# Reading the moving operand of a split product in alternating steps of 16 columns

## Time and profile before

| | |
|---|---|
| median of 3 runs | 2075.34 us (2073.47 to 2078.24) |
| profiled execution, its own time | 2075.21 us |
| its span, first to last instruction | 2073.4 us |
| PE busy | 1975.6 us, 95% of the span |
| PEld busy | 1644.3 us, 79% |
| DVE busy | 1725.3 us, 83% |
| ACT busy | 1328.1 us, 64% |
| read from memory | 557 MB, 269 GB/s over the span |
| mean granted TensorE clock | 0.982 of full |

### The profile page before, as it was taken

How to read it: one execution, slowest core, us unless ns; L and a number is a source line. 1 busy time by engine, 2 the same in 40 slices (tenths; PEclk the granted TensorE clock), 3 DMA queues, 4 the chain that set the end, 5 groups by cost and what they waited for, 6 DMA issues and landing times.

```text
span 2073.4 us, 28446 instructions
## 1 busy us (share of the span) xinstructions
PE 1975.6 (95%) x10316; PEld 1644.3 (79%) x10316; DVE 1725.3 (83%) x2440; ACT 1328.1 (64%) x1977; POOL 0.2 (0%) x4
## 2 busy tenths in 40 slices
PE   6998999989989999999999999999999998999997
PEld 5777889978877788788888878888888876767785
DVE  7798878768776698989989898998989988785764
ACT  4353534355564587788788787888878774554543
POOL 0000000000000000000000000000000000000000
PEclk9999999999999999999999999999999999999999
DMA  9856689846332298999999999999989994672630
GB/s 378 300 170 234 229 301 327 287 142 207 116 111 82 91 382 325 359 334 382 366 351 365 329 368 345 374 352 340 371 325 377 380 354 158 222 247 68 217 122 21
DMA packets 154211, 560.19 MB, mean 270 GB/s; under 512 B 17232, under 2 KB 17488, under 8 KB 153936
## 3 DMA queue, kind: packets, MB, share of 16 engines
q1 hardware_dynamic: 154064, 558.29, 74.1%
HBM read 557.18 MB, written 1.05 MB: 269 GB/s over the span
## 4 chain that ended last, share of the span: by engine, by line
PE 78%; DVE 12%; ACT 5%; issue 3%; DMA 2%; DVEq 0%; SPq 0%; ACTq 0%
PE ps L527 22%; PE ps L529 22%; PE ps L528 22%; PE ps L533 10%; DVE spl L516 3%; PE ps L537 3%; DVE macc L580 2%; ACT sph L504 2%; DMA ring<-in_hyb_w_in 1%; DVE arena L2169 1%; DMA ring<-in_dense_down 1%; ACT arena L771 1%; ACT arena L2135 0%; DVE hL L884 0%; ACT ps L890 0%
## 5 line engine op out<-in xcount | busy, mean ns | idle before, releaser
L504 ACT ACTIVATE sph<-ring 128x1024 fp32r<-128x1024 f32 x906 | 949.2, 1059 | 517.0 <-PE ps L529 332.8
L516 DVE TENSOR_TENSOR spl<-ring,sph 128x1024 fp32r<-128x1024 f32 x906 | 1078.2, 1219 | 241.5 <-ACT sph L504 229.0
L527 PE MATMUL ps<-sph,hH 128*128 128x512 f32 (+1 forms) x1296 | 522.6, 403 | 1.4 <-DVE hL L884 1.3
L529 PE MATMUL ps<-sph,hL 128*128 128x512 f32 (+1 forms) x1296 | 507.8, 392 | 0.0
L528 PE MATMUL ps<-spl,hH 128*128 128x512 f32 (+1 forms) x1296 | 506.9, 391 | 0.0
L529 PEld LDWEIGHTS ps<-sph,hL 128*128 128x128 f32 x1296 | 245.5, 189 | 52.6
L527 PEld LDWEIGHTS ps<-sph,hH 128*128 128x128 f32 x1296 | 246.4, 190 | 51.3 <-issue 3.8
L528 PEld LDWEIGHTS ps<-spl,hH 128*128 128x128 f32 x1296 | 246.4, 190 | 48.4 <-issue 1.0
L527 PE MATMUL ps<-sph,rH 128*128 128x512 f32 x664 | 269.1, 405 | 5.9 <-ACT arena L3123 2.3
L529 PE MATMUL ps<-sph,rL 128*128 128x512 f32 x664 | 259.9, 391 | 0.0
L528 PE MATMUL ps<-spl,rH 128*128 128x512 f32 x664 | 259.4, 391 | 0.0
(11 more groups left out here) (317 smaller groups left out, 1754.4 us busy)
## 6 DMA issues: line engine op xcount, KB each, us to landing
ring<-in_moe_gu SPq DMA_DIRECT2D x448, 512.0 KB, 5.4
ring<-in_moe_down SPq DMA_DIRECT2D x224, 512.0 KB, 5.3
ring<-in_mod SPq DMA_DIRECT2D x144, 512.0 KB, 5.0
ring<-in_w_in SPq DMA_DIRECT2D x64, 512.0 KB, 4.5
ring<-in_dense_gu SPq DMA_DIRECT2D x44, 512.0 KB, 5.3
ring<-in_ssm_w_in SPq DMA_DIRECT2D x40, 512.0 KB, 4.2
ring<-in_dense_down SPq DMA_DIRECT2D x22, 512.0 KB, 5.4
ring<-in_hyb_w_in SPq DMA_DIRECT2D x20, 512.0 KB, 5.9
```

Of the source, the lines that this page charges most:

```text
L504: a.activation(k.high[m % SPLITS][:, 0:w], raw[:, 0:w], ACT.Copy).then_inc(k.S.half_rounded, 1)
L516: v.tensor_tensor(k.low[m % SPLITS][:, 0:w], raw[:, 0:w], k.high[m % SPLITS][:, 0:w], ALU.subtract).then_inc(*k.tick(k.S.half_split, f"hal ...
L527: pe.matmul(out, a[0], b[0], start=start, stop=False, skip_group_check=True)
L529: return pe.matmul(out, a[1], b[0], start=False, stop=stop, skip_group_check=True)
```

## The change

`mm3` passes the output and the two moving operands through a new function `paced`. Where the width is a multiple of 256, it reads the columns in another order: the operand is cut in two halves (`j`), each half in steps of 16 columns (`n`), and the steps are taken from the last to the first, at each of them the one of the lower half and then the one of the upper half. Inside a step the 16 columns go upwards. For 512 columns the order is 240 to 255, 496 to 511, 224 to 239, 480 to 495, and so on to 0 to 15, 256 to 271. The output gets the same order, so that each column of the product lands where it did. At 296 columns nothing changes. The stationary operand, the number of matmuls, all waits, counters and transfers, and the products by `mm` and `turn` stay as they are.

```
+def paced(ap):
+
+    return ap.rearrange("p (j n i) -> p n j i", j=2, i=16)[:, ::-1] if ap.shape[1] % 256 == 0 else ap
+
+
 def mm3(pe, out, a, b, start, stop):
-    pe.matmul(out, a[0], b[0], start=start, stop=False, skip_group_check=True)
-    pe.matmul(out, a[0], b[1], start=False, stop=False, skip_group_check=True)
-    return pe.matmul(out, a[1], b[0], start=False, stop=stop, skip_group_check=True)
+    out, high, low = paced(out), paced(b[0]), paced(b[1])
+    pe.matmul(out, a[0], high, start=start, stop=False, skip_group_check=True)
+    pe.matmul(out, a[0], low, start=False, stop=False, skip_group_check=True)
+    return pe.matmul(out, a[1], high, start=False, stop=stop, skip_group_check=True)
```

## The result

| | before | after |
|---|---|---|
| median of 9 runs | 2073.47 us (2068.16 to 2078.24) | 2089.64 us (2079.18 to 2096.09) |
| ratio | | 1.0071, interval 1.0055 to 1.0087 |
| profiled execution | 2075.21 us, span 2073.4 | 2089.69 us, span 2087.9 |

The change costs about 15 us. That is inside the predicted range of 2005 to 2165 us, but not in the likeliest case (no change, within 4 us): it is the side that got 0.30.

What follows compares the result with a forecast made beforehand. PE, busy 95%, was taken as the bound, through `mm3`'s matmuls; 7752 matmuls x 0 ns = 0 added to span 2073.4 plus 1.8 us around it gave 2075.2, forecast 2075.5 us, range 2005 to 2165 us.

Steps and rivals of the forecast that it cites:

- the likeliest case: All 7752 changed matmuls: nothing in the stream changes, 2071 to 2080 us; chance 0.40.
- the side that got 0.30: Whole kernel slower by more than 0.2%: 0.23 for a cycle's worth per jump plus 0.07 for the lower rate.
- The contention with ACT and DVE that I excluded: In the experts: starts stay 226.7 ns apart with DVE 92% and ACT 81% busy, so no visible contention to heal.
- fixed part: At each matmul's start: 13.3 ns for the split product, about 2.5 ns in plain float32; costed unchanged.
- what a jump costs: Between column runs in the changed matmuls: taken as 0 ns, upper end 1.7 ns, +356 us if all showed.
- the score product: Attention scores of the first token tile: two runs of 128, one jump, 215 ns each, leaving 0 to 1.7 ns per jump.
- the weights for the next one are loaded behind it just as before: At each changed matmul's start: weight loading stays as it was, so no change in cost.
- The rival "faster": At each changed matmul's start: two reads no longer meet, saving 11 ns; 65 us less, 2010 us; chance 0.30.
- The second rival: In the changed matmuls: each jump costs one array cycle, 12.9 or 6.3 ns per matmul; +87 us, 2163 us; chance 0.23.
- whole lines carry no penalty: On both sides of each changed matmul: runs of 16 float32 are 64 bytes, whole lines, so no penalty.

Runs made afterwards that it cites:

- the two measurements: Bare kernels of fixed float32r matmuls, no reference computed, operands' starting places shifted; paced, stationary operand 16 columns on, took 227.9 ns in one and 236.9 in the other.
- the scan: In a bare matmul kernel, the stationary operand started 0 to 60 columns on; at 512 columns plain took 226.7 to 234.0 ns, paced 226.8 to 228.8 from 20 to 48.

## Why the range held and the mechanism did not

**What held.** What bounds the kernel: the split product's matmuls, one after the other, with nothing in reserve in the experts. Waits gave back a few us (about 4 of 20). No instruction, wait or transfer moved. The contention with ACT and DVE that I excluded wasn't there. That the time lies in the range is owed to its width, which was laid out for a cycle per jump and for a shrinking fixed part, and neither came. By the forecast's own check, "the forecast is wrong if the distance moves by more than an array cycle at either width", it is wrong: the distance moved by 3.6 ns, over eight cycles, at 512 columns, and by 0.8 ns, two cycles, at 256.

**The step that failed** is "what a jump costs": 0 ns, from the score product with its one jump of 128. It has two faults. The row was at two cycles per column, which I had named as its weakness. And it asked the wrong question: a jump has no price of its own (steps of 64: none; backward, without a jump: 6 ns). What the change cost, 3.6 ns at each matmul of 512 columns, depends on how the moving operand's order and place stand to those of the weights, and no single product of the trace could have shown it.

**That "the weights for the next one are loaded behind it just as before"** passed over the place of the weights, on which the price turned. The rival "faster" had the mechanism, two reads that meet, but I argued against it from 13.3 ns being "the same whatever lies where" in two stages. Both stages have every operand of `mm3` at the same place modulo 64 columns (all these buffers are multiples of 64 columns long, and so are the steps within them), so that they were one observation and not two. And I took from that mechanism only a gain, not that a new order may meet worse.

**The second rival** had the sign right, and the size and the mechanism wrong: +87 us for one cycle per jump, in the ratio 31 to 15. Measured: 20 us in the stream, 3.6 ns at 512 columns and 0.8 at 256, a ratio of over 4 and not 2.

**The Trainium skill's two sentences.** The Trainium skill's page "PSUM — Partial Sum Buffer", section "Specifications (TRN2)", says that any non-contiguous pattern slows matmuls significantly. The runs disagree for an output in runs of 16 columns: with the output alone in steps the group settles at the plain pace, 226.9 ns. The Trainium skill's page "SBUF — State Buffer", section "Door 1: The DMA port swizzle", says that consecutive accesses to the same 16-byte line run at full bandwidth, and the prediction concluded that whole lines carry no penalty. That came true of steps of 64, not of steps of 16, 8 or 4 (the last being one whole line) with the halves in turn, which cost 6 to 25 ns a matmul at 512 columns.

**What is shown and what is argued.** Shown: the moving operand's side, no contention with ACT or DVE, a dependence on the weights' place relative to it for plain and paced, and that moving the buffers turns the sign in the whole kernel. That the two reads meet in the memory is argued. For it speaks that the extra of paced goes when fewer weights are loaded; against it that the fixed part doesn't, that the order upwards costs 13 ns wherever the weights stand, and that the two measurements disagree at the same place by up to 9 ns. How they meet stays open.

## What to carry to other kernels

Before an order of reading is judged, vary where the operands stand: a change of access pattern and a change of allocation are one experiment, and each alone may show a gain or a loss of 1% that belongs to the pair. A bare measurement of many groups in one kernel costs a single run and told in advance what most of the full kernels did; look at the settled pace of a group and not at its mean, place the group twice behind different neighbours, and carry over only groups in which both operands stand as in the kernel. And two rows that share a hidden condition (here, every operand a multiple of 64 columns from the next) are one piece of evidence.

## What the runs showed that I had not expected

- At the full clock a float32r matmul of 512 columns took from 226.7 to 266.3 ns by the order of its moving operand and output (266.3: columns backward within steps of 16, in the scan), at 213.3 ns for one cycle per column.
- At 256 columns the plain kernel's 120 ns isn't the floor: 113.3 ns with paced and the weights 20 to 48 columns on.
- Three settled paces recur to a tenth in many groups at 512 columns, 226.7, 233.3 and 240.0 ns: 6.7 ns or 16 array cycles apart. Others lie between them (228.3, 230.0, 236.7).
- A run of like matmuls is not steady from its start: plain groups needed up to ten distances of 224 to 241 ns before they stood at 226.7.
- Allocation alone, with the same instructions, moved the whole kernel by 0.8%.
